# Attention steps alternated one by one with half-size pieces of the output product, in a two-block transformer kernel

## The reference

```
proj = x @ w_in                      # qf kf vf (8 heads x 64), gate, cq (512), ckv (256), kr (32)
o_fox = attention(qf, kf, vf, decay) # heads 0 to 7 below ("fox")
q  = rms_norm(cq)  @ w_uq            # 8 heads x (64 + 32 rotary)
kv = rms_norm(ckv) @ w_ukv           # 8 heads x (64 key + 64 value)
o_mla = attention(q with rope, [k, rope(kr)], v)   # heads 8 to 15 below ("mla", latent)
h = concat([o_fox, o_mla]) @ w_out   # 1024 x 1024, the output product
x = layer_norm(ALPHA * x + h)        # then a feed-forward part begins
```

## Time and profile before

| what | value |
|---|---|
| time, median of 3 runs | 978.26 us (978.03 to 978.44) |
| the profiled execution: time, span | 977.55 us, 975.7 us |
| PE busy | 945.5 us, 97% of the span |
| DVE, ACT, POOL busy | 646.3 us (66%), 466.6 us (48%), 60.8 us (6%) |
| mean granted TensorE clock | 0.998 |
| the odd layer's steps named above | about 379 to 474 us of the span |

### The profile page before, as it was taken

One profiled execution on the slowest core, in us unless ns is written; L12 is line 12 of the kernel. 1 busy time (PEld: TensorE's weight loads), 2 busy tenths in 40 slices (PEclk: granted clock), 3 DMA queues, 4 the chain that ended last, 5 costly groups with the idle time before them and its releaser, 6 DMA issues.

```text
span 975.7 us, 15125 instructions
## 1 busy us (share of the span) xinstructions
PE 945.5 (97%) x6537; PEld 864.5 (89%) x6537; DVE 646.3 (66%) x737; ACT 466.6 (48%) x577; POOL 60.8 (6%) x79
## 2 busy tenths in 40 slices
PE   6999999999999999899899999999899999999997
PEld 6999889999999899776699989998899889999986
DVE  4966896545354873676659778789766865555554
ACT  6546844434343465755544343445354544444442
POOL 2024000000000000220030000000000000000000
PEclk9999999999999999999999999999999999999999
DMA  8743385655555454312579999995565456565531
GB/s 262 239 151 130 111 273 184 206 177 177 199 186 173 131 173 114 130 44 87 187 281 326 393 313 335 313 345 175 182 199 188 132 177 210 176 203 183 175 127 44
DMA packets 122282, 190.52 MB, mean 195 GB/s; under 512 B 6566, under 2 KB 103080, under 8 KB 119144
## 3 DMA queue, kind: packets, MB, share of 16 engines
q1 hardware_dynamic: 115184, 156.94, 49.5%
q0 software_dynamic: 5616, 31.78, 9.0%
q10 hardware_dynamic: 1416, 0.83, 0.3%
HBM read 188.49 MB, written 1.05 MB: 194 GB/s over the span
## 4 chain that ended last, share of the span: by engine, by line
PE 70%; DVE 9%; ACT 3%; issue 2%; DMA 1%; DVEq 0%; POOL 0%
PE PS L567 13%; PE PS L565 13%; PE PS L566 13%; PE PS L572 9%; PE PS L574 9%; PE PS L573 9%; DVE lo L1576 2%; ACT hi L1137 1%; PE PS L701 1%; DVE stats L1653 1%; PE PS L665 1%; DVE r L1646 1%; ACT hid L1438 1%; DVE x_tok L1666 1%; DVE gate_s L2007 1%
## 5 line engine op out<-in xcount | busy, mean ns | idle before, releaser
L1576 DVE TENSOR_TENSOR lo<-raw,hi 128x2048 fp32r<-128x2048 f32 (+2 forms) x150 | 336.4, 2258 | 167.3 <-ACT hi L1137 167.1
L565 PE MATMUL PS<-x_hi,hi 128*128 128x256 f32 x1320 | 375.2, 284 | 1.5 <-DVE x_lo L1773 1.5
L567 PE MATMUL PS<-x_hi,lo 128*128 128x256 f32 x1320 | 373.0, 283 | 0.0
L566 PE MATMUL PS<-x_lo,hi 128*128 128x256 f32 x1320 | 372.5, 282 | 0.0
L1137 ACT ACTIVATE hi<-raw 128x2048 fp32r<-128x2048 f32 (+2 forms) x150 | 278.1, 1880 | 10.5 <-DMA raw<-even_w_in 6.6
L565 PEld LDWEIGHTS PS<-x_hi,hi 128*128 128x128 f32 x1320 | 252.1, 191 | 3.9 <-DVE lo L1576 1.9
L566 PEld LDWEIGHTS PS<-x_lo,hi 128*128 128x128 f32 x1320 | 252.1, 191 | 1.9 <-issue 0.5
L567 PEld LDWEIGHTS PS<-x_hi,lo 128*128 128x128 f32 x1320 | 252.0, 191 | 0.0
L572 PE MATMUL PS<-hi,hid_hi 128*128 128x512 f32 x352 | 141.2, 401 | 0.7 <-DVE hid_lo L1847 0.5
L574 PE MATMUL PS<-hi,hid_lo 128*128 128x512 f32 x352 | 138.6, 394 | 0.0
L573 PE MATMUL PS<-lo,hid_hi 128*128 128x512 f32 x352 | 138.5, 394 | 0.0
(11 more groups left out here) (280 smaller groups left out, 824.9 us busy)
## 6 DMA issues: line engine op xcount, KB each, us to landing
raw<-ffn_w_gate SPq DMA_DIRECT2D x22, 1024.0 KB, 5.4
raw<-ffn_w_up SPq DMA_DIRECT2D x22, 1024.0 KB, 5.6
raw<-ffn_w_down SPq DMA_DIRECT2D x22, 1024.0 KB, 5.0
raw<-mlp_w_in SPq DMA_DIRECT2D x16, 1024.0 KB, 5.6
raw<-mlp_w_out SPq DMA_DIRECT2D x16, 1024.0 KB, 4.9
sq<-ada_w POOLq DMA_DIRECT2D x12, 1024.0 KB, 6.3
r<-ada_w POOLq DMA_DIRECT2D x12, 1024.0 KB, 7.0
raw<-sc_w_in SPq DMA_DIRECT2D x12, 1024.0 KB, 5.2
```

What stands on the lines that cost most here:

```text
L565: pe.matmul(dst, wh, hi, start=start, stop=False, skip_group_check=True)
L566: pe.matmul(dst, wh, lo, start=False, stop=False, skip_group_check=True)
L567: return pe.matmul(dst, wl, hi, start=False, stop=stop_, skip_group_check=True)
L1576: dve.tensor_tensor(split_view("lo", c), split_view("raw", c), split_view("hi", c).bitcast(F32), ALU.subtract)\
```

## The change

It does three things. The four pieces `rows` of 12 matmuls become eight of 6 matmuls (one half of the tokens each), and two more pieces of 6 are cut out of the tail (`rows` 8 and 9: the first token half of chunk base+16). They stand in the list after steps 7 to 14, 16 and 18, one behind each. The fills are spread differently: `kvn_sum` comes before `uq 0`, `uq 1` before step 5, step 6 between the fills `q1` and `k2`, step 7 after the last fill. Before, steps 6, 7 and 8 stood at these three places (after `uq 1`, after `q1`, after the last fill). The three splits of the output weights stand after steps 8, 11 and 14.

```diff
-            ("proj", 10), ("att", 3), ("uq", 0), ("kvn_sum", 0), ("att", 4), ("kvn_out", 0), ("att", 5), ("uq", 1),
-            ("att", 6)] + [("mla", i) for i in range(5)] + [("att", 7)] + [
-            ("mla", i) for i in range(5, 11)] + [("att", 8), ("rows", 0), ("att", 9), ("rows", 1), ("att", 10), ("att", 11),
-            ("att", 12), ("rows", 2), ("att", 13), ("att", 14), ("rows", 3), ("att", 15), ("att", 16), ("att", 17), ("att", 18)]
+            ("proj", 10), ("att", 3), ("kvn_sum", 0), ("uq", 0), ("att", 4), ("kvn_out", 0), ("uq", 1), ("att", 5)] + [
+            ("mla", i) for i in range(5)] + [("att", 6)] + [("mla", i) for i in range(5, 11)]
+        for _a in range(7, 15):
+            ODD_STEPS += [("att", _a), ("rows", _a - 7)]
+        ODD_STEPS += [("att", 15), ("att", 16), ("rows", 8), ("att", 17), ("att", 18), ("rows", 9)]
+        OUT_SPLITS = {8: 15, 11: 16, 14: 17}
...
-                q, kk = i // 2, i % 2
-                if kk == 0:
+                q, kk, h = (i // 4, i // 2 % 2, i % 2) if i < 8 else (2, i % 2, 0)
+                c = first["odd_out"] + q
+                if i % 4 == 0:
                     pe.wait_ge(sem("odd_evac"), 21)
                     pe.wait_ge(sem("qm_rot"), 4)
                     pe.wait_ge(sem("o_lo"), 2 * q + 2)
-                rows_part(first["odd_out"] + q, x_hi[:, 2 * q:2 * q + 2, :], x_lo[:, 2 * q:2 * q + 2, :], kk, q == 0, b0=4)
-
+                    pe.wait_ge(lo_split, c + 1)
+                t = slice(h * P, (h + 1) * P)
+                for n in range(2):
+                    last = tok3(PS[:, 4 + 2 * h + n, :], c, slice(n * HB, n * HB + HB), kk, x_hi[:, 2 * q + kk, t],
+                                x_lo[:, 2 * q + kk, t], q == 0 and kk == 0, False)
+                if q < 2 and kk and h:
+                    last.then_inc(chunk_used, 1)
...
             for h in range(2):
-                rows_half(first["odd_out"] + 2, x_hi[:, 4:6, :], x_lo[:, 4:6, :], h, b0=4)
+                if h:
+                    rows_half(first["odd_out"] + 2, x_hi[:, 4:6, :], x_lo[:, 4:6, :], h, b0=4)
                 rows_end(first["odd_out"] + 3, x_hi[:, 6:8, :], x_lo[:, 6:8, :], h, "odd_out", b0=4)
...
-                if a in (7, 8, 12):
-                    split(base + {7: 15, 8: 16, 12: 17}[a])
+                if a in OUT_SPLITS:
+                    split(base + OUT_SPLITS[a])
```

## The result

The changed kernel takes **987.24 us** (median of 6 runs, 985.91 to 988.22), the kernel before 978.96 us (6 runs, 978.03 to 980.59) beside it: a ratio of 1.0089, 95% interval 1.0078 to 1.0100. It is slower by 0.9%, where 982.3 us was forecast and 985.2 us was the upper end. The profiled execution took 988.22 us with a span of 986.3 us, 10.67 us more than that of before (977.55 and 975.7), and a granted clock of 0.987 in the mean instead of 0.998. With the ratio the change costs 8.7 us, where +4.1 us was forecast.

A forecast was written before the change was run, and what follows sets the result against it. PE was taken to set the pace, with holes spent waiting for DVE, directly or through ACT. Terms -0.7 + 3.9 + 0 + 0.9 = +4.1 us, added to the median, gave 982.3 us; range 978.2 to 985.2.

The forecast's parts named there:

- Fills and steps 3 to 7: Early part: three gains (0.8, 1.6, 0.8 us) against 2.5 us more hole before `k1`; sum -0.7 us.
- The hole before `k1`: PE would reach this fill early and wait for DVE's `kr_sum`: 3.1 us instead of 0.64.
- Steps 8 to 18: Half pieces cover the splits too little: holes of 1.25, 1.0 and 3.35 us; the part costs +3.9 us.
- The 8.53 us: Time from a step's start on PE until DVE, after a split, has scaled that head's probabilities; used to size three holes.
- 0.5 us booked as covered by `rows` 8: Between last transpose and tail: an old hole of 0.55 us would be covered, so 2.92 us becomes 2.4.
- Tail and norm: PE's tail has 12 matmuls fewer, but DVE's chain releases the norm: gain 0.
- The clock: One stretch at half clock, after PE's quiet around the norm's transposes: +0.9 us, bounds 0 and 3.4.
- the one it feared behind step 14: Hole of 3.35 us on PE before head 14's transpose, which might bring a second half-clock stretch.
- Rival 3: Two clock stretches, the second from the hole after step 14: +6.6 us, 984.9 us, chance 0.12.
- what would show it: Signs listed beforehand: PE's holes and their sizes, tail start about 3 us later, PE idle before the norm's transposes, then half clock.
- the fills reach the last one more than 2 us earlier: Sign that the forecast is wrong: PE gets to the last latent fill over 2 us sooner than before.

The follow-up runs named there:

- busy_holes: The changed kernel with unread matmuls on PE: six before `k1`, seven before head 14's transpose, four before the norm's transposes; 982.29 us, ratio 1.0042.
- the versions put together: Four kernels with half pieces, an early feed-forward split and differing early orders, against the kernel before; ratios 1.0031, 1.0004, 0.9994 and 0.9990.
- before_busy: The kernel before with four unread matmuls in front of the norm's transposes; 979.62 us, ratio 1.0014.
- busy_k1_only: The changed kernel with six unread matmuls in front of `k1` alone; 985.10 us, ratio 1.0067.
- tail_whole: The changed kernel with the ninth and tenth half pieces back in the tail, which has its 48 matmuls again; 984.43 us, ratio 1.0071.
- k1_busy: The kernel before with the new order of the fills and six unread matmuls in front of `k1`; 978.61 us, ratio 1.0007.

## Why the forecast was right in kind and wrong in size

- **Fills and steps 3 to 7** (forecast -0.7). Without clock loss, in busy_holes, step 8 begins at 440.46 (441.12 less the 0.66 to its transpose), 1.44 of it `rows` 0: 1.55 us earlier than 440.57. The hole before `k1` is right within 0.2 us; the part gained 0.85 us more than summed.
- **Steps 8 to 18** (forecast +3.9). In busy_holes DVE's splits begin at 479.13, 38.67 us after step 8's start, against 34.56 before; with `rows` 0 it is +5.55, 1.6 more than forecast. The 8.53 us held (475.20 - 466.62 = 8.58 for step 14 in the changed kernel). What was missed: ACT's 0.64 us behind the second hole, 0.07 us more in each half-piece step, and 0.5 us booked as covered by `rows` 8: from the last transposes to the splits it took 4.19 us, and 4.24 before. The hole went and the chain from attend to `x_lo` and split did not.
- **Tail and norm** (forecast 0): right; the chain behind the splits is 8.69 us in both.
- These make +4.0 us against a forecast of +3.2; busy_holes shows 4.2 us in its profiled execution and 4.1 by its ratio. The holes are explained. The two misses, -0.85 and +1.6, partly cancel. That busy_holes takes 982.29 us, the very number forecast, is luck: it loses no clock there, and the forecast has 0.9 us of it.
- **The clock** (forecast +0.9, bound 3.4) is the term that failed. It expected one stretch of 3.4 us behind the norm, and as a bound one more behind step 14. There were three, of 6.8, 3.4 and 6.9 us: 6.0 us in the profiled executions, 4.6 us by the ratios. Twice the length at two places was not thought of, and one place was left out: the forecast had itself worked out a hole of 3.1 us before `k1`, as long as the one it feared behind step 14, and put no clock on it. The price per us (0.26) was near the measured 0.3 to 0.4.
- Rival 3 (two clock stretches, 984.9 us, 0.12) named the mechanism and was still too small. The range ended 0.3 us above its value and left no room for a third.
- Of "what would show it", the holes came true, down to the PE idle before the norm's transposes. Two lines did not: "a stretch at 0.50 after it" should have been three, and with their loss the first piece behind step 18 (`rows` 9) starts at 481.16, 7.35 us later than 473.81 and not about 3; in busy_holes it is 476.80, 3.0 later. One of the signs of being wrong was badly chosen: "the fills reach the last one more than 2 us earlier" holds in busy_holes (435.34 against 439.06) without speaking against the forecast, since step 7 (1.87 us) now stands behind the last fill and the forecast's own sum gives 2.6.

## What to carry to other kernels

Price a hole of PE twice, its length and what it may do to the granted clock, and do it for every hole of that size in the new order, not for the one looked at last: here holes of 2 to 3.3 us each brought 3.4 to 6.9 us at 0.50, and their clock cost as much as all the holes' net length. Before moving work out of a tail or into a chain, find out what ends together there; where two engines end together, an improvement of one alone brings nothing. A few unread matmuls in a hole that no order removes gave back half of the loss; where PE does not wait they only cost. Price the early and the late part of a new order apart: in the versions put together the late part gave its 1.8 us and the early part gave nothing or lost.

## What was not expected of the hardware

- The granted clock fell behind holes of 2.93 and 3.25 us although PE was busy on both sides of them, and in single executions behind shorter ones too: at 415.9 in that of before_busy, for 3.4 us, behind holes of 1.27, 0.99 and 0.64 us. PE's quiet is not all that decides it, and what else does stays open. The hole of head 14, 3.25 us in each, is followed by 3.4 us at 0.50 in the changed kernel, by 6.8 us in busy_k1_only and by 10.2 us in tail_whole (from 472.0).
- A stretch at 0.50 need not cost anything that can be seen: that at 687.6 to 691.0 in the kernel before is missing in k1_busy, and from the norm's transposes to the end of the span it takes 490.9 us with it and 491.4 without. The DMA share there is 0.60 to 1.08, and PE waits in it anyway.
